# Two-block transformer on one core: stationary weights 64 bytes into their ring slots, and a softplus six units earlier

## What is computed

```python
def first_block(x, ...):
    u = rmsnorm(h, attn_norm_w[l])
    z, xbc, dt_raw, q, kc, vc, ks, vs, kw, vw, gate_raw = jnp.split(u @ w_in[l], split_at, axis=-1)
    y_ssd = ssd_mixer(z, xbc, dt_raw, ...)     # dt = softplus(dt_raw + dt_bias)
    y_att = nsa_mixer(q, kc, vc, ks, vs, kw, vw, gate_raw, ...)
    h = h + concatenate([y_ssd, y_att]) @ w_out[l]
    v = rmsnorm(h, ffn_norm_w[l])
    h = h + (silu(v @ w_gate[l]) * (v @ w_up[l])) @ w_down[l]
def second_block(x, ...):
    ...  # again u @ w_in, a gated recurrence, an attention, w_up, w_o, and a feed-forward of width 5632
```

## Time and profile before

| | |
|---|---|
| median of 3 runs | 2555.56 us (2555.49 to 2556.26) |
| profiled execution | 2555.69 us, its span 2553.9 us |
| PE busy | 2544.0 us (100%), 13432 matmuls |
| PEld busy | 2121.1 us (83%) |
| DVE, ACT, POOL busy | 1513.2, 1248.7, 53.6 us |
| DMA | 202 GB/s over the span, 64.5% of the queue's 16 engines |

### The profile page before, as it was taken

The page is one execution under the profiler, slowest core; times in us unless marked ns, Lnnn a source line. Parts: engine busy times, 40 slices in busy tenths (PEclk is TensorE's granted clock), DMA queues, the critical chain, the costliest instruction groups (busy, mean ns, idle before and its releaser), DMA issues.

```text
span 2553.9 us, 33053 instructions
## 1 busy us (share of the span) xinstructions
PE 2544.0 (100%) x13432; PEld 2121.1 (83%) x13432; DVE 1513.2 (59%) x1809; ACT 1248.7 (49%) x1582; POOL 53.6 (2%) x68
## 2 busy tenths in 40 slices
PE   9999999999999999999999999999999999999998
PEld 9878888888888888888888888888888888888887
DVE  6787776555455545576578554556655544555555
ACT  5576655444344434466455454534644444443443
POOL 0150000000000000000000000000000000000000
PEclk9999999999999999999999999999999999999999
DMA  8643557766676666776655566676577666776664
GB/s 302 179 163 120 173 172 248 222 215 211 193 226 209 212 191 214 216 228 216 190 174 165 166 175 194 186 262 197 197 217 227 209 195 209 216 221 195 208 206 149
DMA packets 172840, 515.03 MB, mean 202 GB/s; under 512 B 17104, under 2 KB 48080, under 8 KB 171632
## 3 DMA queue, kind: packets, MB, share of 16 engines
q1 hardware_dynamic: 172544, 512.77, 64.5%
q10 hardware_dynamic: 144, 0.15, 0.0%
HBM read 492.54 MB, written 19.92 MB: 201 GB/s over the span
## 4 chain that ended last, share of the span: by engine, by line
PE 98%; DVE 1%; ACT 1%; issue 0%; DVEq 0%; ACTq 0%
PE ps L516 97%; PE ps L520 1%; ACT W L1152 0%; DVE wlo L1711 0%; DVE W L1711 0%; ACT L1152 0%; ACT whi L1152 0%; DVE W L2381 0%; DVE h L1714 0%; DVE scr L1711 0%; DVEq L2696 0%; ACT scr L1152 0%; ACT sm L1152 0%; DVE RB L1787 0%; DVE W L2564 0%
## 5 line engine op out<-in xcount | busy, mean ns | idle before, releaser
L1711 DVE TENSOR_TENSOR wlo<-raw,whi 128x1024 fp32r<-128x1024 f32 x884 | 1080.3, 1225 | 946.1 <-ACT whi L1152 941.7
L1152 ACT ACTIVATE whi<-raw 128x1024 fp32r<-128x1024 f32 x884 | 933.8, 1059 | 1071.2 <-PE ps L516 1055.5
L516 PE MATMUL ps<-whi,xx 128*128 128x512 f32 x4160 | 1284.9, 390 | 0.0
L516 PEld LDWEIGHTS ps<-whi,xx 128*128 128x128 f32 x4160 | 777.7, 188 | 160.7 <-issue 0.7
L516 PE MATMUL ps<-wlo,xx 128*128 128x512 f32 x2080 | 809.6, 389 | 0.0
L516 PEld LDWEIGHTS ps<-wlo,xx 128*128 128x128 f32 x2080 | 390.4, 188 | 81.5
L516 PE MATMUL ps<-whi,hlo 128*128 128x512 f32 x944 | 368.6, 390 | 0.0
L516 PE MATMUL ps<-whi,hhi 128*128 128x512 f32 x944 | 367.4, 389 | 0.0
L516 PE MATMUL ps<-wlo,hhi 128*128 128x512 f32 x944 | 367.3, 389 | 0.0
L516 PE MATMUL ps<-xx,whi 128*128 128x512 f32 (+1 forms) x1088 | 310.8, 372 | 0.1
L516 PEld LDWEIGHTS ps<-xx,wlo 128*128 128x128 f32 x960 | 180.3, 188 | 37.9 <-DVE wlo L1711 1.2
(11 more groups left out here) (168 smaller groups left out, 916.5 us busy)
## 6 DMA issues: line engine op xcount, KB each, us to landing
raw<-in_gu SPq DMA_DIRECT2D x352, 512.0 KB, 4.3
raw<-in_w_in SPq DMA_DIRECT2D x256, 512.0 KB, 4.1
raw<-in_dn SPq DMA_DIRECT2D x176, 512.0 KB, 4.2
raw<-in_w_out SPq DMA_DIRECT2D x32, 512.0 KB, 3.7
raw<-in_w_up SPq DMA_DIRECT2D x32, 512.0 KB, 4.2
raw<-in_w_o SPq DMA_DIRECT2D x32, 512.0 KB, 4.3
W<-blocks SPq DMA_DIRECT2D x120, 128.0 KB, 2.7
blocks<-W SPq DMA_DIRECT2D x20, 512.0 KB, 6.3
```

What stands on the lines that cost most here:

```text
L516: return e.matmul(o, l, r, start=start, stop=stop, skip_group_check=skip)
L1152: return e.activation(o, i, f, **kw)
L1711: return e.tensor_tensor(o, a, b, op)
```

## The change

It has two parts. First, each slot of `whi` and `wlo` becomes 1056 floats long (4224 bytes), and in items of the kinds "feat" and "half" the 1024 floats of a unit begin 16 floats (64 bytes) into the slot; in all others at its start. `first_unit` takes its views from `slot(0)`, so that it follows. Second, `gates` waits 29 units instead of 35 on both engines.

```diff
-        whi = sb("whi", [P, NSPL, 1024], R)
-        wlo = sb("wlo", [P, NSPL, 1024], R)
+        whi = sb("whi", [P, NSPL, 1056], R)
+        wlo = sb("wlo", [P, NSPL, 1056], R)
...
-            return whi[:, q % NSPL, :], wlo[:, q % NSPL, :]
+            o = 16 if units[q]["item"]["kind"] in ("feat", "half") else 0
+            return whi[:, q % NSPL, o:o + 1024], wlo[:, q % NSPL, o:o + 1024]
...
-                wh = whi[:, 0, :].rearrange("p (k n) -> p k n", n=CH)
-                wl = wlo[:, 0, :].rearrange("p (k n) -> p k n", n=CH)
+                wh, wl = (w.rearrange("p (k n) -> p k n", n=CH) for w in slot(0))
...
-                yield from later(35)
+                yield from later(29)
                 yield from softplus(1, 32, 1)
...
-                yield from later(35)
+                yield from later(29)
                 yield from softplus(1, d32, 32, False)
```

## The result

| | before | changed |
|---|---|---|
| median | 2555.52 us (2555.47 to 2556.26, 4 runs) | 2588.96 us (2588.48 to 2589.75, 4 runs) |
| span of the profiled execution | 2553.9 us | 2588.0 us |
| PE busy | 2544.0 us | 2573.7 us |

The ratio is 1.013 with a 95% interval of 1.0113 to 1.0148: 33.4 us were lost where 0.6 were to be gained. The time lies outside the range of the prediction.

The account below looks back on a forecast made before the run. TensorE bounds the kernel, its time a sum of matmul start distances. From the profiled 2555.69 us, 0 (64 bytes) + 0 (ring) - 0.64 (stall) gave 2555.0, or 2554.9 against the median; 8-in-10 range 2543 to 2559.

Parts of the forecast that it names:

- rest: In TensorE's start distances, time beyond streaming the columns: 13.4 ns in tok, 13.3 in feat, 14.3 in half.
- The 64 bytes: Moved stationary weights of feat and half, 2048 matmuls: 0 us, bounds 10.9 us less to 8.2 us more.
- thin items: Items with 256-column matmuls, fixed places: 116.5 ns with 128- and 64-column loads, 115.5 with 16 and 8; used as evidence.
- Rival 1: Stationary load's place matters at 64 bytes and helps: 4 ns on 2048 matmuls, 2546.7 us; chance 0.38.
- The ring: 4224-byte slots put tok weights in slots 1 and 3 128 bytes off (modulo 256): 0 us, bounded at 18.
- Rival 2: Slower by the ring: tok in slots 1 and 3, 4 ns on 4536 matmuls, 18 us, 2573 us; chance 0.08.
- cmp: Items whose stationary operand runs through all multiples of 32 bytes: 116.4 ns mean, 4 ns spread; evidence that place costs nothing.
- The rule on TensorE's two read ports: Skill's rule of separate moving and stationary ports: an operand's place costs nothing, same 0; not needed for the sum.
- The stall near 250 us: End of compressed attention, TensorE waiting 0.48 us for ScalarE's eviction: goes when the softplus moves, gain 0.64 us.
- The new place of the softplus: Item 1x1, 3.0 us more ScalarE work: costs 0; if the chain is 1 us short, about 1 us stall per reader.
- The two readers that I followed: TensorE's uses at 225.22 and 226.24 us, after ScalarE's eviction and VectorE's copy: margins 1 and 0.8 us, no stall.
- rival 3: Slower by the 64 bytes themselves: 4 ns up on 2048 matmuls, less 0.64, 2562.4 us; chance 0.06.

Follow-up runs that it names:

- e3: Kernel before with only the 64 bytes for feat and half, in 4352-byte slots, softplus still at 35 units: 2552.56 us, ratio 0.999.
- e8: Kernel before with 4352-byte slots, all kinds of weights beginning 0 to 60 bytes in, in steps of 4, softplus at 35: 2603.50 us, one execution.
- e2: Kernel before with only the slots widened to 4224 bytes, all weights at a slot's start, softplus at 35: 2587.97 us, ratio 1.0128.
- e12: The whole change with one number different, slots of 4352 bytes in place of 4224: 2557.65 us, ratio 1.0008 to the kernel before.
- e5: Kernel before with 4352-byte slots, all weights and `xx` 128 bytes further, `hhi` and `hlo` kept in place modulo 256: 2571.96 us, one execution.
- e1: Kernel before with only the softplus moved, after 29 units instead of 35, ring as before: 2560.14 us, ratio 1.0019.
- e10: Kernel before with 4352-byte slots, feat and half weights at 64 bytes, softplus after 40 units instead of 35: 2551.77 us, ratio 0.9987.
- e6: Kernel before with softplus at 29, its `Exp`, `Ln` and the `Exp` of `a_log` made copies, so no table loads for them: 2558.44 us.

## Point by point: what of the prediction held

- **What bounds the kernel.** Held: the time is the sum of TensorE's start distances, and the "rest" over the columns is the only thing that an address changes. It changed.
- **The 64 bytes, taken at 0 (bounds -10.9 and +8.2).** Within the bounds, wrong in the value taken. "Feat" fell by 6.7 ns, beyond the 4.5 that I had as its bound from the thin items; "half" by 1.6 in the item shown and by 0.5 (e3) to 0.9 (changed kernel) over all, far from the 5.5. Alone it gives 2.9 us (e3). The 4.5 ns that I put down to the length of the load may have been the place as well: in e8 "feat", with full loads of 128 columns, takes 115.5 ns at 8 bytes, the same as the loads of 16 and 8 columns. Rival 1 had the mechanism, at 8.2 us nearly three times its size.
- **The ring, taken at 0 (bound 18 us).** This is the step that failed: the inference from "256 bytes apart costs nothing" to "128 bytes apart costs nothing". It cost 31 to 32 us, in e2, by e12 and in the changed kernel. Rival 2 had mechanism, place (half the "tok" units) and sign, at a chance of 0.08 and 4 ns a matmul, where a matmul in a bad slot loses 5.8 ns and one in a good slot behind it 1.3 on average. Three inferences under it were wrong.
  - From "tok" at 226.7 both at the same place modulo 512 and 256 bytes apart it took the place to do nothing. The price repeats after 256 bytes, so these two were one sample of the curve, at its floor. At fourteen of the fifteen other multiples of 16 it costs 1.7 ns or more.
  - It set "cmp", at all places, 116.4 ns, beside thin, at fixed ones, 116.5. Two means that agree don't say that their parts do. "Cmp" differs from "tok" in who is long, in the length of the load (120 and 60 columns) and in the columns that move; in a "tok" stream, places that were really varied average 232 against 227.
  - It took the spread of "cmp", 4 ns, as a bound. That was read from starts printed to 10 ns, on another shape. Measured, a place costs up to 13 ns (20 bytes).
- **The rule on TensorE's two read ports.** The Trainium skill, SBUF — State Buffer, "Who interferes with whom", gives TensorE two independent read ports and has it wait for nobody; the prediction drew from it that a place costs nothing. The runs go against that for this kernel: moving both operands costs nothing, moving one costs 5.7 ns (e5). The prediction's sum did not need the rule, but took the same 0.
- **The stall near 250 us, -0.64.** Held: gone in the changed kernel, in e1 and in e10.
- **The new place of the softplus, taken at 0.** Wrong: +5.3 us before that gain. The two readers that I followed do not wait, as worked out. But I stopped there. All that stands behind the moved operations on VectorE is late too, and it had only 1.15 us of idle time to catch up in ahead of the third reader, the multiply that frees the bank of the scores. The 1 us that it allowed for a chain that is too short bounded the error of the chain, not of where it ends. That a stall of 4 us would cost clock on top (2.1 us here) was not in it either.
- **The range.** It left out the one rival whose price was largest and whose row of before did not exist. No row of before had a stationary 128 bytes off its moving operand in a long stream; for a term of 4536 matmuls that is a reason for a wide range, not for 0.08. Two slips beside that decide nothing: the 2562.4 of rival 3 takes the 0.64 off twice (2555.6 + 8.2 - 0.64 is 2563.2), and 2543 lies below the bound of 2544.0, not nearly at it.

## What to carry over

If a slot's length or a tensor's place changes, work out for every matmul stream the byte distance between moving and stationary operand, slot by slot, and ask whether any slot had that distance before; if none did, the cost is unknown, and it is multiplied by all matmuls of the stream. Here lengthening slots by 256 bytes was free and by 128 cost 31 us. When an operation is moved on an engine that has little idle time, follow the queue behind it until the idle time has paid the delay back, and look at each release on the way, those of PSUM banks too, not only at the operations named in the change.

## What the runs showed of the hardware

- Distances of a dense stream of 128x512 matmuls with 128-column loads: 226.7 ns at the best place, up to 240 at the worst; the byte distance of the operands modulo 256 sets it, and 4 bytes can change it by as much as 9 ns. The order of the values (4 bytes 236.6, 12 bytes 228.9, 20 bytes 239.9, 28 bytes 226.8) shows no pattern that I can name, and what in the chip makes it stays open.
- The best place of the weights differs by kind: 64 bytes in, weights that move lose 2.5 ns (229.2), stationary ones under 256-column matmuls gain 6.7 ("feat", 113.3), and in "half" some distances gain and others lose. No run separates who moves from the length of the matmul. So a unit's place can be chosen by kind, as the change does, but only if the ring leaves it there.
- After 2.5 us (e6) and 4 us without a matmul the granted clock of TensorE stood at 0.50, the lower level, for some 3 to 6 us of the work that followed, while the stall of 0.5 us at 250 us left it at 1.00. That work lost 1.0 us in e6, 1.3 in e1 and 2.1 in the changed kernel, so a stall of 4 us costs 5.3 to 6.1 here.
